# Prompt attention of a decoder step: probabilities turned by a product with a scaled diagonal, in place of a scale and a transpose

## The reference, cut to what matters

```python
s = jnp.where(mask, s.astype(jnp.float32), MASK_NEG)
e = jnp.exp(s - jnp.max(s, axis=-1, keepdims=True)) * mask
return e / jnp.maximum(jnp.sum(e, axis=-1, keepdims=True), 1e-30)
...
oc = jnp.einsum('bghtj,bjgd->btghd', pc.astype(vc.dtype), vc)
...
return g[..., 0:1] * oc + g[..., 1:2] * osel + g[..., 2:3] * ow
```

## Time and profile before

| | us |
|---|---|
| median of 3 runs | 2573.42 |
| lowest and highest run | 2568.65, 2578.06 |
| the profiled execution | 2577.74 |
| its profiled span | 2575.9 |
| the prompt attention in it (first scores to last copy of heads) | 248.9 to 450.2 of the span, some 201 |

### The profile page before, as it was taken

One profiled execution on the slowest core, in us unless ns is written; L12 is line 12 of the kernel. 1 busy time (PEld: TensorE's weight loads), 2 busy tenths in 40 slices (PEclk: granted clock), 3 DMA queues, 4 the chain that ended last, 5 costly groups with the idle time before them and its releaser, 6 DMA issues.

```text
span 2575.9 us, 30760 instructions
## 1 busy us (share of the span) xinstructions
PE 2367.5 (92%) x11201; PEld 1784.4 (69%) x11201; DVE 1267.6 (49%) x3256; ACT 637.6 (25%) x1463; POOL 234.5 (9%) x459
## 2 busy tenths in 40 slices
PE   6998999888868999999999899888959999999996
PEld 5636555666657888888887565645748888888884
DVE  2013887555127777778322400165067777777223
ACT  1002877444122222221001210212112222220003
POOL 0002000000001222221000000020002222220000
PEclk9997999999988999999999999955969999999998
DMA  7116400695312323232221312130022322222221
GB/s 165 49 33 204 95 2 2 176 231 154 61 30 77 98 66 98 66 98 66 82 82 33 91 49 65 34 99 5 0 74 68 96 71 94 72 92 78 83 69 44
DMA packets 200408, 203.14 MB, mean 79 GB/s; under 512 B 38630, under 2 KB 188718, under 8 KB 199934
## 3 DMA queue, kind: packets, MB, share of 16 engines
q1 hardware_dynamic: 197010, 183.70, 25.1%
q0 software_dynamic: 3248, 17.47, 2.3%
HBM read 192.00 MB, written 17.46 MB: 81 GB/s over the span
## 4 chain that ended last, share of the span: by engine, by line
PE 85%; DVE 8%; issue 3%; DMA 1%; ACT 1%; SPq 0%; DVEq 0%; POOL 0%; ACTq 0%; POOLq 0%
PE PS L2023 48%; PE PS L1947 7%; PE PS L1300 5%; PE PS L1970 4%; PE PS L1323 3%; PE PS L1936 2%; PE PS L589 2%; PE PS L603 2%; PE PS L663 2%; PE PS L621 1%; DVE RR L2322 1%; DMA ring<-in_w_ffn_up 1%; PE PS L651 1%; PE PS L677 1%; PE PS L1293 1%
## 5 line engine op out<-in xcount | busy, mean ns | idle before, releaser
L2023 PE MATMUL PS<-HT,ring 128*128 128x272 f32 x1536 | 376.7, 395 | 16.9 <-DVE HT L2332 16.9
L2023 PEld LDWEIGHTS PS<-HT,ring 128*128 128x128 f32 x1536 | 293.9, 191 | 77.9 <-issue 17.0
L2023 PE MATMUL PS<-arena,ring 128*128 128x272 f32 x1392 | 341.5, 392 | 0.0
L2023 PEld LDWEIGHTS PS<-arena,ring 128*128 128x128 f32 x1392 | 264.5, 190 | 54.5
L2219 ACT ACTIVATE arena<-arena,CB,CW 128x560 f32<-128x560 f32 x128 | 109.2, 853 | 386.3 <-DVE arena L2450 319.5
L2023 PE MATMUL PS<-arena 128*128 128x272 f32 x768 | 191.8, 393 | 0.4 <-DVE arena L2392 0.4
L2023 PE MATMUL PS<-arena,CONST 128*128 128x272 f32 x768 | 191.7, 392 | 0.0
L1947 PE MATMUL PS<-HT,ring 128*128 128x272 f32 x768 | 182.4, 401 | 7.5 <-DVE HT L2332 5.3
L2465 DVE SCALAR_TENSOR_TENSOR arena<-arena,CW 128x560 f32<-128x560 f32 x256 | 187.3, 789 | 0.0
L1947 PEld LDWEIGHTS PS<-HT,ring 128*128 128x128 f32 x768 | 149.5, 195 | 40.0 <-issue 6.5
L2023 PEld LDWEIGHTS PS<-arena 128*128 128x128 f32 x768 | 145.8, 190 | 31.7 <-issue 1.8
(11 more groups left out here) (392 smaller groups left out, 3200.6 us busy)
## 6 DMA issues: line engine op xcount, KB each, us to landing
ring<-in_w_ffn_up SPq DMA_DIRECT2D x64, 1024.0 KB, 8.4
ring<-in_w_ffn_down SPq DMA_DIRECT2D x32, 1024.0 KB, 5.0
ring<-in_cache_nsa_kv SPq DMA_DIRECT2D x128, 128.0 KB, 4.1
arena<-in_cache_nsa_kv SPq DMA_DIRECT2D x56, 256.0 KB, 7.0
ring<-in_w_ml_in SPq DMA_DIRECT2D x12, 1024.0 KB, 5.5
arena<-in_cache_nsa_win SPq DMA_DIRECT2D x16, 512.0 KB, 5.4
out_nsa_win_sample<-in_cache_nsa_win POOLq DMA_DIRECT2D x8, 1016.0 KB, 15.3
ring<-in_w_nsa_in SPq DMA_DIRECT2D x6, 1024.0 KB, 5.4
```

Of the source, the lines that this page charges most:

```text
L2023: last = mm(PS[:, bank, 0:HALF], lhs[:, k, :], rhs(k), start=(first and k == 0), stop=(done and k == 3))
```

## The change

The scale of the unit on DVE is gone. In its place DVE writes, for each unit, a 128 x 128 diagonal with reciprocal times gate on it into `DG`, four buffers in the last plane of `HT`. PE then multiplies each block of `PB`, as stationary operand as before, by this diagonal with `mm`: the block comes out turned and scaled at once. Before it writes a diagonal, DVE waits on `s_tp` until the unit that used the buffer four units ago has been turned.

```diff
+        DG = HT[:, KT - 1, 0:4 * P].rearrange("p (s c) -> p s c", s=4)
+
...
                     if br == 0:
-                        last = tr(PS[0:NCMP_P, 4 + g2, 0:P], PB[:, u % 6, 0:NCMP_P], ident)
+                        last = mm(PS[0:NCMP_P, 4 + g2, 0:P], PB[:, u % 6, 0:NCMP_P], DG[:, u % 4, :], start=True, stop=True)
                     else:
                         for k in range(i + 1):
-                            last = tr(PS[:, 4 + g2, k * P:(k + 1) * P], PB[:, u % 6, k * P:(k + 1) * P], ident)
+                            last = mm(PS[:, 4 + g2, k * P:(k + 1) * P], PB[:, u % 6, k * P:(k + 1) * P], DG[:, u % 4, :],
+                                      start=True, stop=True)
                     last.then_inc(s_tp, 1)
...
-                    v.tensor_scalar(PB[:, u % 6, 0:w], PB[:, u % 6, 0:w], st[:, 2, g2:g2 + 1],
-                                    G[:, i, c:c + 1], ALU.mult, ALU.mult).then_inc(s_sc, 1)
+                    if p >= 2:
+                        dve.wait_ge(s_tp, u - 3)
+                    v.tensor_scalar(DG[:, u % 4, :], ident, st[:, 2, g2:g2 + 1], G[:, i, c:c + 1], ALU.mult, ALU.mult)\
+                        .then_inc(s_sc, 1)
```

More of the change, by code:

```diff
@@ L1050, in weighed @@
                 n, i, br = PAIRS[p]
-                w = unit_width(br, i)
                 st = ST[:, p % 4]
```

## The result

The changed kernel takes 2602.65 us at the median of 4 runs (2600.86 to 2606.46), the kernel before 2575.74 of 4 (2568.65 to 2578.63). The ratio is 1.0111, with a 95% interval of 1.0085 to 1.0136: slower by 27 us. The forecast was 2613, slower by 40, with a range of 2597 to 2626. So the sign and the mechanism came out, and the growth was forecast half as large again as it was, 40 us for 27.

What follows compares the result with a forecast made beforehand. TensorE was taken to bound the kernel, with VectorE counting only at late places: 49.2 us of added work less 7.7 hidden less 1.6 for a cold stretch, about +40 on 2573.42, so 2613 us, range 2597 to 2626.

Steps and rivals of the forecast that it cites:

- The count: TensorE, prompt attention: an fp32 product is two instructions, a transpose one, so 768 in place of 384.
- The price of one: TensorE, prompt attention: one instruction of a plain product costs 0.1115 us, one transpose 0.108 us.
- The rival of four for one: TensorE's turning: a product costs four times a transpose, 0.432 us, giving 2680 us; chance 0.02.
- The first load of a group: TensorE's turning groups: the first weight load, hidden by nothing, takes 0.049 us more, 3.1 us over 64 wide pairs.
- The sum of TensorE's work: Prompt attention: TensorE's work grows by 49.2 us, 46.8 of it before the charges for first loads and half-speed clock.
- What is hidden: Where TensorE idled for VectorE's late scale, added work is free: 0.96 us a head pair, 7.7 us in all.
- A: Place in a head pair around the copy of finished heads; TensorE's idle time there goes from 1.47 to 1.04 us.
- B: Place in a head pair after the biases of the 512-wide tile; TensorE's idle time goes from 0.73 to 0.36 us.
- The clock: Prompt attention: work done at half clock costs 2.4 us more; one of three cold stretches goes, 1.6 us less.
- the rival on the clock: Prompt attention: plain products keep the clock up where transposes did not, so +34 us, 2607; chance 0.08.
- Nothing behind takes it back: Behind the prompt attention: the sample's attention starts from the last copy of heads, so the growth reaches the end.
- The rival on the faster side: Prompt attention: VectorE sets the pace and products are one instruction each, so 9.9 us less, 2563.5; chance 0.03.

Runs made afterwards that it cites:

- e3_turn_twice: The kernel before with every transpose of the probabilities issued twice in a row into the same place; 1.0119 of the kernel before.
- e5_narrow_wait: The kernel before with 128-wide diagonals written in place of the scales and the new wait, blocks still transposed with the unit matrix; 0.9985 of before.
- e7_later_and_fill: The kernel before with the copy of finished heads in step 10 of twelve, not 4, and four filling transposes each at A and B; 0.9962 of before.
- e9_fill_idle: The kernel before with eight filling transposes ahead of TensorE's late group at A, four at B, and two waits reordered; 0.9991 of before.
- e1_narrow_only: The kernel before with 128-wide diagonals written in place of the scales, without the new wait, blocks still transposed with the unit matrix; 0.9989 of before.

## Why the prediction was right, and where it was off

**The count.** Right, and it decides everything: 640 and 128 instructions. e3_turn_twice shows that the count alone is 4.33 of the 4.83 us a head pair that products cost.

**The price of one.** Right. 0.111 us against 0.1115 forecast from L1978, and 193 ns for a load against 194. The rival of four for one did not come: two instructions of a product take 0.222 us and one of a transpose 0.108, a ratio near two. The Trainium skill gives four passes through the array for a true fp32 product ("FP8 and Floating Point Precision", TensorE Precision Notes). No trace counts passes, so that figure is not refuted; the prediction's step from it to four times a transpose is.

**The first load of a group.** Right, some 0.05 us in each.

**The sum of TensorE's work.** Nearly right. The groups of a head pair grew, by the chain: 0.75 twice for the 384-wide pairs, 0.96 twice, 0.50 twice, 0.27 twice for the 128-wide ones, 0.21 four times for branch 0. That is 5.8 us; 46.8 / 8 = 5.85 was forecast at the full clock.

**What is hidden.** The first of the terms that were off. The forecast left 1.04 us of idle time at A and 0.36 at B; the trace has 0.92 and 0.31. Its own terms say why: 0.05 us for each wait was charged, three times on the way, and e5_narrow_wait shows it free. VectorE's half alone was to save 0.08 us a head pair with waits or 0.23 without, and saved 0.32. So some 1.2 us a head pair are taken up in place of 0.96, a head pair grows by 4.60 and not by the 4.9 that the forecast makes at the full clock, and that is 2.4 us in all.

**A step that was missing.** At place B the chain now runs over ACT: its exponentials of an earlier pair (323.49, L895 x4) start only when the long group of products before them is turned and copied, and VectorE then waits for them. VectorE waits for ACT about once a head pair in both kernels. Timeline of VectorE, before:

```profile
320.86 0.06 DVE L1043 MEMSET turn<- 1x1 f32 x1 [1.02 <-ACT arena L892]
```

and after:

```profile
325.00 0.06 DVE L1046 MEMSET turn<- 1x1 f32 x1 [1.11 <-ACT arena L895]
```

Before, that wait fell behind place B, 4.9 us after the late group at 315.96 had started, and nobody waited for VectorE there. After, it falls just ahead of the late group at 326.89. I had written that ACT would fall further behind the bound: it is busy for 20.2 of 28.57 us, and yet it comes last at B. What it costs is small, since TensorE idles there for 0.31 us only; no run takes it apart.

**The clock.** The second and the third. I took it that one of three cold stretches would go, 1.6 us. All three went: the same 1.6 us for each, 4.7 in all. And 2.4 us were charged for products done in the cold, in those three and in the first ten microseconds. The latter came in both kernels, so their price can be looked up, in windows from one head pair's first scores to the next one's; the first head pair and the last, before:

```profile
248.93:274.09 25.16, 22.51 (x165) 12.98 (x165) 19.91 (x116) 17.56 (x67) 0.00 (x0) 0.80 0.96 252
...
421.01:450.17 29.16, 26.44 (x222) 16.06 (x220) 21.09 (x119) 21.59 (x79) 0.00 (x0) 0.94 0.01 2
```

and after:

```profile
248.56:277.94 29.38, 27.36 (x205) 18.74 (x205) 19.53 (x117) 18.32 (x67) 0.00 (x0) 0.83 0.97 246
...
449.37:481.79 32.42, 31.06 (x278) 22.41 (x276) 19.62 (x118) 22.06 (x78) 0.00 (x0) 1.00 0.01 2
```

The first head pair, which has the ten microseconds at half the clock, grew by 4.2 us, less than the 4.6 of an undisturbed one; the last by 3.3, or 4.9 without the cold stretch that it had before. So nothing of the 2.4 us is seen; why products cost no more in the cold start is not shown. On the cold stretches the rival on the clock came true, and by the density of the work, not by its kind.

Together: the stage was to grow by 39.9 us and grew by 32.0. 2.4 of the 7.9 are the hidden work, 3.1 the two further cold stretches, and 2.4 the cold charge.

**Nothing behind takes it back.** Right for the work, and the profiled execution still shows 8.5 us less behind the stage. The instructions there are the same, and so is TensorE's order. Behind the stage the ten profiled executions of this study take 2117.2 to 2125.7 us, the kernel before being at the upper end (with e7_later_and_fill) and the change at the lower. The profiled execution of before also lies 2 us above its median and that of after 1.8 below, so the medians differ by 27 where the executions differ by 23. The four runs of the changed kernel themselves spread over 5.7 us of span, 2599.0 to 2604.7, with mean clocks of 0.943 to 0.939. The clock accounts for the 8.5 us. By its records in the traces, TensorE was at half the clock for 271.8 us behind the stage before and for 254.5 after; at 1.6 us for a cold stretch, 3.4 us long in these records, the 17.3 us less are 8.1 us of time. Over all ten executions that time lies between 254 and 272 us, and with half of it taken off, the part behind the stage takes 1988.0 to 1993.0 us in every one, 1989.8 before and 1990.0 after. So the work there did not change. Nor does the little time at half the clock need the products: e9_fill_idle, without them, has 254.1. Why it differs between executions stays open; as far as the prediction goes it is chance, and no more than a hint at why the median grew by 27 us where the stage grew by 32.

**The rival on the faster side** had its point of decision at 2.2 us a head pair of additional work on TensorE. The work is 5.8. e1_narrow_only shows what would be left of it if TensorE's work did not grow: 0.32 us a head pair, within what can be measured of no change.

## What to carry to other kernels

Before a transpose is traded for a product, count instructions in the trace: in fp32 a call of the product is two instructions with two weight loads, a call of the transpose one, and where the chain runs over TensorE the difference is paid there; here 4.6 of the 5.8 us a head pair. Work saved on a second engine is worth only what lies at the places where the first one waits for it, here 0.32 of 0.9 us a head pair. Look at such a place for other work that stands in the late engine's queue: moving a copy of 0.68 us out of it gained more than the whole saving of the change could have.

## What the runs showed of the hardware that was not expected

- Idle time filled with transposes keeps TensorE at the full clock, 1.00 for 185 us in e9_fill_idle against 0.97 before. That kernel's median shows no gain, since its head pairs are 0.25 us longer, most of it at places without a filling, where the edit changed only the order of two waits.
- The additional wait ahead of VectorE's diagonals costs nothing that the head pair shows: 23.65 us with and without. The unit that it waits for has been turned by then, and the first diagonal of a pair comes behind a reciprocal of the same engine.
- A cold stretch of 3.3 us costs its head pair 1.6 us, and how many a stage has changes between executions of nearly the same code: three in before, five in e1_narrow_only and three shorter or longer ones in e5_narrow_wait, where both have the same head pair of 23.65 us. Behind the stage it is the same: 254 to 272 us at half the clock in ten executions, with the same instructions. A difference of 5 us in a profile of this kernel is no sign of anything until the clock's column has been read.
